# Last layer without its context rows, tokens kept on chip between two written-out layers, and modulation on four column tiles

## The chip, the cores and the metric

One Trainium2 chip, one core. The metric is the device time of one execution in microseconds (us); lower is better. In the traces PE is TensorE (matmuls; PEld its weight loads), DVE is VectorE, ACT is ScalarE, POOL is GpSimd and SP is SyncE, which here only issues DMAs.

## The reference

Two layers of a token mixer. 256 context tokens and 1024 latent tokens have 1024 channels each. A layer computes, with everything in float32:

```
for l in range(2):
    sh, sc, gt = split(silu(c) @ w_mod[l] + b_mod[l])          # latents; context tokens use silu(c_ctx)
    h = rmsnorm(x, norm_g[l]) * (1 + sc) + sh                  # ctx likewise
    p = h @ w_in[l]                                            # columns are split among the four head groups
    y = concat(diff_attention, mlstm, gla, window_gqa)         # each reads context and latents
    y = y * silu(p[gate columns])
    x = x + gt * (y @ w_out[l])
    if l == 0: ctx = ctx + gt_c * (yc @ w_out[l])              # only the first layer
return x
```

In the last layer the context tokens are keys, values and recurrent state for the latents. Their own mixed rows, gates and output are not used after it.

## The kernel before

Tokens come in NT = 10 tiles of 128: two of context (NC = 2), eight of latents. `hT` [128, 8, 1280] holds the modulated input by channel, `yT` of the same size the mixed output. Weights come as 18 slabs a layer through `ring`, two buffers of up to 2 MB (`load_slabs`, L158): SP loads slab i once slab i-2 has been used, which is counted in `slab_used`.

`layer_program` (L98) runs `setup`, and then a hardware loop over two layers. Each stage is a block of five programs, one for each engine, synchronized by semaphores, and a barrier of all engines that clears them ends it. The stages of a layer, in this order:

- `setup` (L175, once): loads the constants and c, copies the 5.24 MB of tokens from the input to the buffers `ctx_now` and `out` in DRAM, waits for all four transfers, and only then forms silu(c).
- `stage_modulation` (L204): SP loads the parameters `par` (1.18 MB), slabs 0 and 1, ten token tiles of 0.5 MB into `yT`, then slabs 2 to 7. PE multiplies each of slabs 0 to 5 (512 columns) by silu(c), 2 columns wide, in 8 float32 matmuls, which are 16 instructions (L241); ACT keeps each result (L262). Meanwhile ACT squares and sums the token tiles (L267), and ACT and DVE scale them (L277, L295). At the end PE turns the 2-row result into columns (L248), DVE adds the gate's bias (L300), PE spreads the gate rows over 128 partitions (L254), and ACT keeps them (L283).
- `stage_norm` (L314): PE transposes the scaled tokens (L346), ACT and DVE write `hT` with scale and shift.
- `stage_mlstm` and `stage_gla`, each closed by `turn_out` (L879), which normalizes the heads' rows and transposes them into `yT`, ten tiles.
- `stage_diff_attention` (L1565): projections, and for each of two pairs of heads `attend_pair` (L1583): 20 units (tile, head). Each unit has two score maps; DVE takes the maximum (L1719), ACT the exponential (L1690). A context tile has 256 keys, a latent tile 1280. Then `turn_out`.
- `stage_window_attention` (L1774): projections and 20 units (tile, group) of 256 to 640 keys (L1924 is the maximum).
- `stage_gates` (L1959): 5 groups of 256 gate columns, 8 steps (128 input channels) each. A step splits `hT` and the weights into high and low float32r parts (ACT L2023; DVE L353, L354, L2056) for PE, which does three matmuls (L2001 to L2003) for each of 2 column blocks by token blocks of 512, 512 and 256. A group has NA = 6 sums in a ring of 8 banks of PSUM: the first step of a group waits until sum n-8 has been read (`made`). ACT takes the sigmoid, DVE multiplies (L2040), POOL multiplies into `yT` (L2068).
- `stage_output` (L2074): 4 groups (column half, token half) of NA = 5 tiles, 8 steps each with 15 matmuls of 512 columns (L2120 to L2122). DVE multiplies the sum by the gate row (L2139), POOL adds it to the residual (L2164), ACT issues the store (L2170). The residual tiles come from DRAM through NB = 4 buffers: the load of tile i waits for the store of tile i-4 (L2106). 20 tiles of 256 KB.

All of this runs over all ten tiles in both layers.

## Time and profile before

| | us |
|---|---|
| median of 2 runs (2875.21 to 2882.43) | 2878.82 |
| the profiled execution, its device time | 2880.83 |
| the profiled execution, span from first to last instruction | 2878.9 |
| PE busy | 2266.4 (79%) |
| DVE busy | 1941.6 (67%) |
| ACT busy | 1203.8 (42%) |
| POOL busy | 426.7 (15%) |
| mean granted clock of TensorE, share of 2.4 GHz | 0.885 |

The device time is the metric; the profiled execution is one more run, 0.07% above the median, and its device time lies 1.9 us above its span. Busy shares are averages over stages that have different limits, so they say little of any one of them. The two layers run the same instructions: the first begins its modulation at 26.26 us and the second at 1452.71 us.

### The profile page before, as it was taken

What the parts mean: (1) busy time and instruction counts of PE and PEld (TensorE: products, weight loads), DVE (VectorE), ACT (ScalarE), POOL (GpSimd) and SP (SyncE); (2) the same over time, 40 slices, a digit from 0 to 9 for tenths busy, and PEclk for the clock granted to TensorE, in tenths of its full rate; (3) what the DMA queues carried; (4) which work ended last, traced back from release to release, by engine and by line L of the source; (5) the groups of instructions that cost most, each with busy time, mean ns of one, the idle gap of its engine ahead of it and who ended that gap; (6) DMA issues with size and microseconds to landing.
All of it is one profiled execution on the core that took longest, in us unless ns stands there. A gap on an engine that the chain in (4) does not pass through costs nothing. (4 is left out here: it accounts for less than half of the span.)

```text
span 2878.9 us, 39611 instructions
## 1 busy us (share of the span) xinstructions
PE 2266.4 (79%) x15156; PEld 1862.1 (65%) x15156; DVE 1941.6 (67%) x3585; ACT 1203.8 (42%) x2248; POOL 426.7 (15%) x422
## 2 busy tenths in 40 slices
PE   4877796786879758898958776977868787488988
PEld 0666685666768636777817666866657686377777
DVE  0476666778979467676715766677889686676766
ACT  2434343333757426442224433433437474364421
POOL 0001303322000030022200012042220000201212
PEclk9988897898989769999989888978989798699999
DMA  8200010000000100001271000100000001000022
GB/s 337 89 15 17 1 59 1 2 0 1 1 1 1 44 30 1 30 30 55 99 287 63 0 18 16 45 1 2 1 1 1 1 1 44 30 1 30 30 79 97
DMA packets 21041, 112.51 MB, mean 39 GB/s; under 512 B 2464, under 2 KB 2464, under 8 KB 15776
## 3 DMA queue, kind: packets, MB, share of 16 engines
q1 hardware_dynamic: 15088, 99.42, 9.2%
q10 hardware_dynamic: 5760, 10.49, 1.0%
q8 instruction: 124, 2.03, 0.3%
q14 instruction: 69, 0.57, 0.1%
HBM read 99.42 MB, written 15.73 MB: 40 GB/s over the span
## 5 line engine op out<-in xcount | busy, mean ns | idle before, releaser
L1719 DVE TENSOR_REDUCE a_st<-ps 128x1 f32<-128x1280 f32 (+1 forms) x160 | 203.5, 1274 | 24.0 <-PE ps L1631 23.1
L1690 ACT ACTIVATE ring<-ps,a_st 128x1280 f32<-128x1280 f32 (+1 forms) x160 | 184.7, 1155 | 76.9 <-DVE a_st L1719 76.3
L2001 PE MATMUL ps<-g_x_hi,g_w_hi 128*128 128x512 f32 (+1 forms) x480 | 175.8, 366 | 29.9 <-DVE g_gate L2040 15.4
L2002 PE MATMUL ps<-g_x_lo,g_w_hi 128*128 128x512 f32 (+1 forms) x480 | 174.8, 364 | 0.0
L2003 PE MATMUL ps<-g_x_hi,g_w_lo 128*128 128x512 f32 (+1 forms) x480 | 172.9, 360 | 0.0
L426 PE MATMUL ps<-a_proj_wh,a_proj_xh 128*128 128x512 f32 (+1 forms) x320 | 118.2, 369 | 65.7 <-DVE a_proj_xl L407 65.7
L2023 ACT ACTIVATE g_x_hi<-hT 128x1280 fp32r<-128x1280 f32 x80 | 101.4, 1272 | 146.3 <-PE ps L2003 139.8
L1631 PE MATMUL ps<-a_k,a_q 128*128 128x512 f32 (+1 forms) x416 | 131.0, 420 | 25.0 <-ACT ring L1690 20.4
L241 PE MATMUL ps<-ring,csil 128*2 128x512 f32 x192 | 92.1, 636 | 73.4 <-DMA ring<-in_w 72.5
L2056 DVE TENSOR_TENSOR g_x_lo<-hT,g_x_hi 128x1280 fp32r<-128x1280 f32 x80 | 119.1, 1489 | 29.4 <-ACT g_x_hi L2023 29.4
L2120 PE MATMUL ps<-o_w_hi,o_y_hi 128*128 128x512 f32 x320 | 125.9, 393 | 16.4 <-ACT o_y_hi L2176 16.4
L1646 PE MATMUL ps<-cst,ring 128*128 128x128 f32 x672 | 109.8, 295 | 29.4 <-ACT a_aT L1699 16.2
L2068 POOL TENSOR_TENSOR yT<-yT,g_gate 128x512 f32<-128x512 f32 (+1 forms) x60 | 66.1, 1124 | 449.5 <-DVE g_gate L2038 262.0
L2122 PE MATMUL ps<-o_w_hi,o_y_lo 128*128 128x512 f32 x320 | 125.5, 392 | 0.0
L2121 PE MATMUL ps<-o_w_lo,o_y_hi 128*128 128x512 f32 x320 | 125.5, 392 | 0.0
L2001 PEld LDWEIGHTS ps<-g_x_hi,g_w_hi 128*128 128x128 f32 x480 | 93.2, 194 | 49.3 <-DVE g_gate L2040 17.9
L390 ACT ACTIVATE b_proj_xh<-hT 128x640 fp32r<-128x640 f32 (+1 forms) x64 | 63.8, 1003 | 140.9 <-PE ps L426 138.5
L426 PEld LDWEIGHTS ps<-a_proj_wh,a_proj_xh 128*128 128x128 f32 x320 | 67.5, 211 | 78.7 <-issue 55.4
L2176 ACT ACTIVATE o_y_hi<-yT 128x640 fp32r<-128x640 f32 x64 | 47.0, 740 | 166.5 <-PE ps L2122 159.1
L426 PE MATMUL ps<-a_proj_wl,a_proj_xh 128*128 128x512 f32 (+1 forms) x320 | 115.2, 360 | 0.0
L426 PE MATMUL ps<-a_proj_wh,a_proj_xl 128*128 128x512 f32 (+1 forms) x320 | 114.7, 358 | 0.0
L1646 PEld LDWEIGHTS ps<-cst,ring 128*128 128x128 f32 x672 | 81.7, 151 | 49.2 <-ACT a_aT L1699 24.0
(358 smaller groups left out, 6533.4 us busy)
## 6 DMA issues: line engine op xcount, KB each, us to landing
ring<-in_w SPq DMA_DIRECT2D x26, 2048.0 KB, 7.6
yT<-latents SPq DMA_DIRECT2D x16, 512.0 KB, 18.6
o_res<-latents SPq DMA_DIRECT2D x32, 256.0 KB, 2.8
latents<-o_res ACTq DMA_DIRECT2D x32, 256.0 KB, 2.4
ring<-in_w SPq DMA_DIRECT2D x6, 1024.0 KB, 4.8
cst<-in_cst SPq DMA_DIRECT2D x1, 2752.0 KB, 8.9
ring<-in_w SPq DMA_DIRECT2D x2, 1312.0 KB, 5.5
par<-in_par SPq DMA_DIRECT2D x2, 1180.0 KB, 5.5
```

Of the source, the lines that this page charges most:

```text
L426: last = pe.matmul(out, left, right, start=k == 0 and j == 0, stop=k == KT - 1 and j == 2)
L1631: last = pe.matmul(ps[:, 3 * c + b, 0:w], q4[:, 2 * h + c, t * P:(t + 1) * P], k4[:, 2 * h + c, k0:k0 + w], start=True, stop=True)
L1646: last = pe.transpose(ps[:, 6 + n % 2, (k - a) * P:(k - a + 1) * P], p(u, 0, T)[:, k * P:(k + 1) * P], C(env, "ident"))
L1690: act.activation(p(u, c, n), ps[:, 3 * c:3 * c + 3, :].rearrange("p b n -> p (b n)")[:, 0:n], ACT.Exp, bias=st[:, 0:1], accum_out=st[:, 1: ...
L1719: dve.tensor_reduce(stat[:, u % SLOTS, c, 0:1], ps[:, 3 * c:3 * c + 3, :].rearrange("p b n -> p (b n)")[:, 0:n], AX.X, ALU.max, negate=Tru ...
L2001: pe.matmul(out, w_hi[:, at, cols], x_hi[:, at, toks], start=k == 0, stop=False)
L2002: pe.matmul(out, w_hi[:, at, cols], x_lo[:, at, toks], start=False, stop=False)
L2003: last = pe.matmul(out, w_lo[:, at, cols], x_hi[:, at, toks], start=False, stop=k == KT - 1)
L2056: dve.tensor_tensor(x_lo[:, at, :], hT[:, k, :], x_hi[:, at, :].bitcast(F32), ALU.subtract).then_inc(split_lo.sem, 1)
L2120: pe.matmul(ps[:, n % 8, :], y_hi[:, at, toks], w_hi[:, at, :], start=k == 0, stop=False)
L2121: pe.matmul(ps[:, n % 8, :], y_hi[:, at, toks], w_lo[:, at, :], start=False, stop=False)
L2122: last = pe.matmul(ps[:, n % 8, :], y_lo[:, at, toks], w_hi[:, at, :], start=False, stop=k == KT - 1)
```

## The change

1. The two layers are written out instead of looped over, and every address is a constant. Stage tensors and semaphores get the layer in their names.
2. In the last layer only the eight latent tiles are kept (`kept_tiles`): in `turn_out` (three times), the units of both attentions, the gates (1024 of 1280 token columns) and the output (8 of 10 tiles). The projections and the scans still run over all ten.
3. `setup` only loads c. The copy of the tokens in DRAM is gone. The first layer reads its tokens from the input, in modulation and again as residual. Order of SP's DMAs: slabs 0 and 1, ten token tiles, `par`, the constants, then slabs 2 to 7.
4. The output stage loads all its residual tiles at once into `hT` (by rows), each with a semaphore of its own, and POOL adds in place. They stay there, so the next layer's modulation reads them without a load; its scaled copy goes to `yT`.
5. In the first layer's output stage SP then loads the next `par`, slab 0 when the splits of the first column half are done, and slab 1 when those of the second are done.
6. Modulation: the eight matmuls of a slab are spread over four column tiles of the PE, k and k+4 sharing one. DVE clears two banks first; ACT keeps all 128 partitions. The turn becomes 16 float32 matmuls that also add the four partial rows (`pair_sum`), it waits for all six slabs, and the gate rows follow at once; their bias is added by DVE as it takes them from PSUM.
7. A second barrier at the end of each layer clears the slab semaphores.

```diff
-        with nc.Fori(0, DEPTH) as layer:
-            env["layer"] = layer
+        for layer in range(DEPTH):
+            env["layer"], env["last"] = layer, layer == DEPTH - 1
...
-                    first = loaded[0].sem.num if stage is stage_output else first_free
-                    nc.all_engine_barrier(sems_to_clear=range(first, first_free + len(stage_sems)))
+                    nc.all_engine_barrier(sems_to_clear=range(first_free, first_free + len(stage_sems)))
+                    if stage is stage_output:
+                        nc.all_engine_barrier(sems_to_clear=range(loaded[0].sem.num, slab_used.sem.num + 1))
...
+def kept_tiles(env):
+    return range(NC if env["last"] else 0, NT)
+def residual_rows(env, t, cols):
+    dram = env["dram"]
+    if env["layer"] == 0:
+        return dram["tok"][t * P:(t + 1) * P, cols]
+    return new_rows(env, t, cols)
...  setup
-            sp.dma_start(env["cst"][:, :], dram["cst"][:, :]).then_inc(const_loaded.sem, 16)
-            sp.dma_start(craw[:, :, :], dram["c"].rearrange("p (k c) -> p k c", k=KT)).then_inc(const_loaded.sem, 16)
-            sp.dma_start(dram["ctx_now"][:, :], dram["tok"][0:CTX, :]).then_inc(const_loaded.sem, 16)
-            sp.dma_start(dram["out"][:, :], dram["tok"][CTX:T, :]).then_inc(const_loaded.sem, 16)
-            sp.wait_ge(const_loaded.sem, 64)
+            sp.dma_start(craw[:, :, :], dram["c"].rearrange("p (k c) -> p k c", k=KT)).then_inc(c_loaded.sem, 16)
+            sp.wait_ge(c_loaded.sem, 16)
...  stage_modulation
+            if first:
+                load_slabs(sp, env, 0, 2)
+                for t in range(NT):
+                    sp.dma_start(x[:, t, :], env["dram"]["tok"][t * P:(t + 1) * P, :]).then_inc(x_loaded[t].sem, 16)
+                sp.dma_start(env["par"][:, :], env["dram"]["par"][0:P, :]).then_inc(par_loaded.sem, 16)
+                sp.dma_start(env["cst"][:, :], env["dram"]["cst"][:, :]).then_inc(env["const_loaded"].sem, 16)
             load_slabs(sp, env, 2, 8)
...
+            pe.wait_ge(cleared.sem, 2)
             for s in range(6):
-                pe.wait_ge(env["loaded"][s].sem, 16)
+                wait_slab(pe, s)
                 if s >= 2:
                     pe.wait_ge(ev.sem, s - 1)
                 for k in range(KT):
-                    last = pe.matmul(ps[0:2, s % 2, :], env["csil"][:, k, :], slab(env, s)[:, k, :],
-                                     start=k == 0, stop=k == KT - 1)
+                    c = k % 4
+                    last = pe.matmul(ps[32 * c:32 * c + 2, s % 2, :], env["csil"][:, k, :], slab(env, s)[:, k, :],
+                                     start=k < 4, stop=k >= 4, tile_position=(0, 32 * c), skip_group_check=True)
...
-            pe.wait_ge(ev.sem, 4)
+            pe.wait_ge(ev.sem, 6)
+            pe.wait_ge(env["const_loaded"].sem, 16)
             for i in range(2 * KT):
-                last = pe.transpose(ps[:, 2, 2 * i:2 * i + 2], rows[:, i * P:(i + 1) * P], C(env, "ident")[0:2, 0:2])
+                last = pe.matmul(ps[:, 2, 2 * i:2 * i + 2], rows[:, i * P:(i + 1) * P], C(env, "pair_sum"), start=True, stop=True)
...  stage_gates
-    NA = GROUP // P * len(BLOCKS)
+    blocks = [(CTX, 512), (CTX + 512, 512)] if env["last"] else BLOCKS
+    T0 = blocks[0][0]
+    NA = GROUP // P * len(blocks)
...
-                act.activation(x_hi[:, i % BUFS, :], hT[:, k, :], ACT.Copy).then_inc(split_hi.sem, 1)
+                act.activation(x_hi[:, i % BUFS, T0:], hT[:, k, T0:], ACT.Copy).then_inc(split_hi.sem, 1)
...  stage_output
-    NA = NT // 2
+    first = kept_tiles(env)[0]
+    NA = (NT - first) // 2
...
             for i, (n, t) in enumerate(jobs):
-                if i >= NB:
-                    sp.wait_ge(x_out[i % NB].sem, 16 * (i // NB))
-                sp.dma_start(res[:, i % NB, :], rows(n, t)).then_inc(x_in[i % NB].sem, 16)
+                sp.dma_start(xs[:, t, cols(n)], residual_rows(env, t, cols(n))).then_inc(x_in[i].sem, 16)
+            if not env["last"]:
+                nxt = slice((env["layer"] + 1) * P, (env["layer"] + 2) * P)
+                sp.dma_start(env["par"][:, :], dram["par"][nxt, :]).then_inc(ahead[0].sem, 16)
+                for i in range(2):
+                    sp.wait_ge(weights.sem, 2 * (i + 1) * KT)
+                    sp.dma_start(env["ring"][:, i, 0:KT * SLAB_W[i]], dram["w"][nxt, SLAB_AT[i]:SLAB_AT[i + 1]])\
+                      .then_inc(ahead[1 + i].sem, 16)
...  turn_out, attend_pair, stage_window_attention (one line of each)
-            for t in range(NT):
+            for i, t in enumerate(tiles):
-    units = [(t, h) for t in range(NT) for h in range(2)]
+    units = [(t, h) for t in kept_tiles(env) for h in range(2)]
-        pairs = [(t, g) for t in range(NT) for g in range(2)]
+        pairs = [(t, g) for t in kept_tiles(env) for g in range(2)]
```

## Rows read from the trace of the kernel before

**Rows 1.** SP's part of the timeline, start of each layer's modulation (start us, us, engine, line).

```profile
26.26 0.35 SPq L224 DMA_DIRECT2D par<-in_par  x1
...
1452.71 0.35 SPq L224 DMA_DIRECT2D par<-in_par  x1
```

**Rows 2.** Timeline of the setup and of layer 1's modulation end.

```profile
25.05 0.22 ACT L194 ACTIVATE csig<-craw 128x16 f32<-128x16 f32 x1 [23.02 <-DMA latents<-in_tok]
...
89.38 0.59 ACT L262 ACTIVATE mod_row<-ps 2x512 f32<-2x512 f32 x1 [6.75 <-PE ps L241]
...
99.00 10.80 PE L346 MATMUL ps<-cst,yT 128*128 128x128 f32 x80 [1.64 <-PEq L138]
```

**Rows 3.** Timeline of layer 2's modulation, 1440 to 1530 us.

```profile
1465.05 8.57 PE L241 MATMUL ps<-ring,csil 128*2 128x512 f32 x16 [22.41 <-DMA ring<-in_w]
...
1511.85 7.03 PE L241 MATMUL ps<-ring,csil 128*2 128x512 f32 x16 [0.31 <-DMA ring<-in_w]
...
1520.90 5.36 PE L254 MATMUL ps<-mod_row,cst 2*128 2x512 f32 x8 [0.76 <-DVE mod_row L300]
...
1527.90 2.37 PE L346 MATMUL ps<-cst,yT 128*128 128x128 f32 x10 [1.63 <-PEq L138]
```

**Rows 4.** Busy time by stretch, layer 2's modulation (stretch, length, engines, PE clock, DMA share, GB/s).

```profile
1474.00:1487.60 13.60, 6.79 (x16) 1.19 (x14) 0.17 (x1) 11.21 (x22) 0.00 (x0) 0.91 1.03 423
```

**Rows 5.** DMA issues of the page: size, median us from issue to landing.

```profile
ring<-in_w SPq DMA_DIRECT2D x26, 2048.0 KB, 7.6
```

**Rows 6.** Timeline: matmuls on two column tiles; weight loads before 64-column matmuls.

```profile
2589.95 1.09 PE L1874 MATMUL ps<-d_aT,d_v 128*64 128x128 f32 x16 [0.48 <-DVE yT L1944]
...
2365.63 2.31 PEld L1661 LDWEIGHTS ps<-yT,ring 128*128 128x128 f32 x20 [0.30 <-ACT a_aT L1699]
```

**Rows 7.** Timeline of differential attention: first maximum, first of a latent unit.

```profile
2149.79 0.76 DVE L1719 TENSOR_REDUCE a_st<-ps 128x1 f32<-128x256 f32 x2
...
2157.41 1.49 DVE L1719 TENSOR_REDUCE a_st<-ps 128x1 f32<-128x1280 f32 x1 [0.82 <-PE ps L1631]
```

**Rows 8.** Timeline of window attention: first maximum, first of a latent unit.

```profile
2499.66 0.42 DVE L1924 TENSOR_REDUCE d_st<-ps 128x1 f32<-128x256 f32 x1 [1.61 <-PE ps L1843]
...
2512.55 0.69 DVE L1924 TENSOR_REDUCE d_st<-ps 128x1 f32<-128x512 f32 x1 [0.39 <-PE ps L1848]
```

**Rows 9.** Timeline of the third turn_out: evictions of ten tiles.

```profile
2389.99 5.27 ACT L934 ACTIVATE yT<-ps,par 128x128 f32<-128x128 f32 x20 [1.24 <-PE ps L918]
```

**Rows 10.** Timeline of the last gates stage, and the start of the output stage.

```profile
2592.44 3.59 ACT L2023 ACTIVATE g_x_hi<-hT 128x1280 fp32r<-128x1280 f32 x3 [3.26 <-PEq L138]
...
2651.94 1.27 ACT L2023 ACTIVATE g_x_hi<-hT 128x1280 fp32r<-128x1280 f32 x1 [2.21 <-PE ps L2003]
...
2655.42 1.27 ACT L2023 ACTIVATE g_x_hi<-hT 128x1280 fp32r<-128x1280 f32 x1 [2.21 <-PE ps L2003]
...
2750.55 0.28 PE L2003 MATMUL ps<-g_x_hi,g_w_lo 128*128 128x256 f32 x1
...
2756.97 1.99 ACT L2176 ACTIVATE o_y_hi<-yT 128x640 fp32r<-128x640 f32 x3 [3.70 <-PEq L138]
```

**Rows 11.** Waits, 2592 to 2757 us: who waited for whom, total us, times, longest.

```profile
PE ps L2001 <- DVE g_gate L2040: 7.7, 3, 2.6
...
PE ps L2001 <- DVE g_gate L2038: 2.9, 2, 1.9
```

**Rows 12.** Costliest groups of the page: DVE's largest operation in the gates.

```profile
L2056 DVE TENSOR_TENSOR g_x_lo<-hT,g_x_hi 128x1280 fp32r<-128x1280 f32 x80 | 119.1, 1489 | 29.4 <-ACT g_x_hi L2023 29.4
```

**Rows 13.** Timeline of the last output stage's start and end.

```profile
2759.03 0.77 PE L2120 MATMUL ps<-o_w_hi,o_y_hi 128*128 128x512 f32 x1 [8.20 <-ACT o_y_hi L2176]
...
2869.02 0.39 PE L2122 MATMUL ps<-o_w_hi,o_y_lo 128*128 128x512 f32 x1
...
2874.24 1.26 POOL L2164 TENSOR_TENSOR o_res<-o_res,o_prod 128x512 f32<-128x512 f32 x1 [1.77 <-DMA o_res<-latents]
```

**Rows 14.** DMA queues of the page: instruction fetch (packets, MB, share).

```profile
q8 instruction: 124, 2.03, 0.3%
```

269 lines of the change are left out of this document (138 added, 131 removed).

## The prediction

> **What bounds the kernel now.** I read the timeline of SP first, because it cuts the run into two layers: modulation begins at 26.26 and again at 1452.71 us [rows 1]. The first layer takes 1426.5 us, and the second, up to the span's end at 2878.9, 1426.2: the same program twice, so a part that leaves one layer is priced from either. The chain of waits only covers the last output stage, so each changed stage is read by itself.
>
> *Setup.* ACT makes silu(c) at 25.05, released by the copy of the latents in DRAM [rows 2]: 25 us in which no engine computes. *Modulation.* PE's first matmul waits until 1465.05 for slab 0, 12.3 us after the stage's start. Then each slab takes 7.03 us of back-to-back matmuls with 0.31 us idle for the next load [rows 3]. PE and the two-slab ring are level, while a stretch where the queues are full moves 423 GB/s [rows 4]: a 2.10 MB slab needs 5.0 us of that, and the issue-to-landing time of 7.6 us [rows 5] leaves 2.6 us of fixed latency. *Gates and output.* In the gates a step comes every 3.48 us and ACT waits for PE each time [rows 10]; PE itself waits 10.6 us in all for DVE to free a bank [rows 11]. In the output stage 480 matmuls fill 2759.03 to 2869.4 without a gap, 3.41 us a step of 15 [rows 13]. Both are bound by PE, so fewer columns shorten them.
>
> **The change part by part.** The sum is made against the profiled execution's 2880.8 us (2.0 above the median).
>
> *Modulation's pace, p us of PE a slab.* The trace shows column tiles on two tiles only: 16 instructions of 128 columns take 1.09 us with the last one's own length in it, about 0.055 us apart [rows 6], while L241 needs 0.44 us for 512 columns on one, or 0.11 for 128 [rows 3]. Two tiles double the pace. Four would give 1.8 us a slab if all overlap, 3.5 if only two at a time do, and twice either at the low clock. The slab matmuls that followed an idle stretch took 8.57 us instead of 7.03, the first ones at half the pace [rows 3]. I take 3.5, with 1.8 and 6.9 as ends.
>
> *Layer 2's modulation.* No token loads, and slabs 0 and 1 are there: slab 1 is issued when DVE has split the last weights, three steps or 10 us before the output's PE end, and needs 7.6. From the start: 1.2 us for DVE's two clears (no row; two reads of 512 columns of PSUM are of that size; 0.3 to 1.2), slab 0 done at 4.7, slab 1 at 8.2. Slab 2 is issued at 4.7 and lands at 12.3, slab 3 5.0 later at 17.3. Slab 4 waits for slab 2's use at 15.8 and lands at 23.4; slab 5 lands at 28.4 and is used up at 31.9. Before, it was at 1518.9, or 66.2. That gives 34.3 us less (38.8 at p = 1.8, 22 at 6.9). ACT's ten squares and two copies, 11.2 us [rows 4], no longer begin behind slab 0's 21 us, and end near 16 us, ahead of slab 4; they hold nobody.
>
> *Layer 1.* c's load is 8 KB, so 2.6 us of latency after 0.8 of issue, and 1.2 us from silu(c) to the stage, as now (25.05 to 26.26): start at 4.6. Ahead of slab 2 lie 4.2 + 5.2 + 1.2 + 2.8 = 13.5 MB. The constants now count here instead of in setup. Slab 2 lands at 4.6 + 2.6 + 15.6 MB / 423 GB/s = 44.0, slab 3 at 49.0, slab 4 (issued at 47.5) at 55.1, slab 5 at 60.1, used up at 63.6. Before it was 89.3 [rows 2]: 25.7 less (28.5 and 17 at the ends of p).
>
> *End of modulation, both layers.* From the last slab to the norm's first transpose: 9.0 us in layer 2 (1518.9 to 1527.9 [rows 3]), 9.7 in layer 1 [rows 2]. The turn is now 32 instructions that each load 128x128 weights. Such loads come every 0.115 us at the full clock [rows 6], so 3.7 us, or 7.4 at half. The 8 gate instructions take 3.4 to 6.9 (5.36 in [rows 3]). With 0.7 for ACT's copy before, 0.7 for DVE's sum after and 1.2 of barrier that is 9.7 to 16.9. I take 13.3, since PE will have been idle half the time: 4.0 us dearer in each layer. PE's gate matmuls no longer wait for DVE's bias, which was 1 us of the old 9.
>
> *Transition.* All residual tiles are there early, so POOL's last add no longer waits 1.77 us for a load, which itself waited for a store [rows 13]: 1.9 us less in layer 1. SP's 20 loads, `par` and slab 0 go past nobody: the output stage's only other DMAs are ACT's stores. The second barrier costs about the 1.3 us that one takes between stages. The loop's own end shows no gap of its own.
>
> *Gates, last layer.* A step has 12 matmuls of 512 instead of 7680 columns: 0.8 x 3.48 = 2.78 us, 27.8 us less in 40 steps. NA = 4 in 8 banks means that a group's first step waits for the group before the last, long read, so the 10.6 us of bank waits go. DVE's largest part shrinks from 1.49 to 1.19 us [rows 12] of a 2.78 us step. At the end four sums at POOL's pace instead of six save about 0.7. Together 39 us. Ends: 28 if the bank waits stay, 40.
>
> *Output, last layer.* 32 steps of 12 instead of 15 matmuls: 32 x 0.68 = 21.8. The end: 9.5 us from the last matmul (2869.4) to 2878.9. New: the first of four sums is ready 2.0 us before PE's end, 0.7 for DVE, four adds of 1.26 [rows 13], and 3.4 us of store as now: 7.1. With 0.2 of smaller splits 24.4 us.
>
> *Attention, last layer.* Four units fall away at the front of each loop. Differential: 2157.41 - 2149.79 = 7.6 [rows 7], less 0.9 for the longer first scores, 6.7, twice: 13.4. Window: 12.9 - 0.9 = 12.0 [rows 8]. *turn_out*, three times: 4 of 20 evictions are 1.05 us [rows 9], and the squares ahead of them, by the same share, about as much again: 5.7 (3.2 to 6.3).
>
> *Sum.* 25.7 - 4.0 + 34.3 - 4.0 + 1.9 - 1.3 + 39 + 24.4 + 13.4 + 12.0 + 5.7 = 147.1. 2880.8 - 147.1 = **2734 us**, 5.1% faster. Some 94 us come from the dropped context rows and 53 from loads and modulation; the tiles alone would be worth little without the loads, since the ring's transfers would take PE's place at 5 us a slab.
>
> **The rivals.** *A: PE stays the bound of modulation.* With idle gaps between slabs PE may run at the low clock all through, and only two tiles may overlap: p = 6.9, so 12.3 us of layer 2's gain and 8.7 of layer 1's are lost, and the end takes 3.6 more in each: 2734 + 28 = 2762. For it: the clock was low in the first matmuls after the idle wait [rows 3]. Against: full clock for most of a stage with short gaps.
> The Trainium skill ("TensorE: Matmul & The Clock Gate", Part 1) says that the throttled state is the default and activity releases it; by that rule layer 2's modulation would be at 1.2 GHz for its whole length. The trace agrees for the stage's start and has no stage with half-idle PE for the rest.
> *B: the last layer's gates and output shrink less than their columns.* If DVE or ACT became the bound in the gates, or bank waits stayed, 11 to 28 us of the 39 would be missing: 2745 to 2762. Against: 1.19 of 2.78 us.
> *C: slower than before, by instruction fetch.* Twice the code, straight through. The fetch queue moves 124 packets [rows 14]. If each now stalled its engine by a landing of 2.6 us, that would be 322 us: 2734 + 322 = 3056. It decides against the change from 147 / 124 = 1.2 us a packet on. Against: a loop's first pass also runs code for the first time, and it took 1426.5 us where the second took 1426.2 [rows 1]; and 2.03 MB fetched is the code of both passes, not of one.
> The skill's page "Runtime: NRT & Kernel Launch", "Instruction fetch mechanics", has straight code prefetched and a far taken branch paying a fetch, so written-out layers would if anything save one such stall; no gap in this trace shows it.
> *D: the change does more.* p = 1.8, a full clock at the end of modulation and shorter attention fill: 2734 - 16 = 2718.
>
> **How the numbers follow.** Forecast as priced 0.62, A 0.16, B 0.10, D 0.10, C 0.01, anything else 0.01. The likeliest case lies within 2722 to 2748. The range takes in D and A: 2713 to 2765; C and a heavier mix of A and B are left out. No change from the median, within 2% (about what a measurement of this kernel can tell from none), begins at 2821 us, which only a sum below 60 us reaches, less than the dropped columns alone give: faster 0.97, same 0.02, slower 0.01.
>
> **What would show it.** Norm's first transpose at about 77 us (before 99.0) and, in layer 2, 45 us after its modulation's start (before 75.2). Slabs of modulation 5.0 us apart with PE waiting for DMA between them. The mixer stages of layer 1 unchanged. Gates 125 us in the last layer (before 164.5), steps of 2.78 us and no PE wait for L2040. Output 97.5 us (before 122). The first maximum of a latent unit follows the scores at once. Wrong would be: PE waits of another kind at the slabs, DVE late in the last gates, idle times named "issue" spread over layer 2.

## The result, and the profile after

The changed kernel took 2726.17 us (median of 2 runs, 2724.24 to 2728.10), the kernel before 2878.82: a ratio of 0.9468, 95% interval 0.9433 to 0.9503. The forecast was 2734 us. The profiled execution took 2724.24 us with a span of 2722.4, which is 156.5 us less than the span before; the prediction's sum was 147.1.

Cut at the first instruction of each stage that it priced, the two spans differ like this. Each length is the difference of two starts in the timelines.

```
stretch                                        before    after   measured  predicted
start to norm's first transpose, layer 1         99.0     78.5     -20.6     -21.7
from there to layer 2's modulation             1353.7   1349.5      -4.3      -0.6
layer 2's modulation, to the norm                75.2     45.7     -29.5     -30.3
from there to the last gates (norm, mixers)    1064.5   1024.4     -40.1     -31.1
last gates                                      164.5    125.1     -39.4     -39.0
last output stage                               121.9     99.3     -22.6     -24.4
sum                                                             -156.5    -147.1
```

**Start of layer 1.** The timeline of the start answers to [rows 2]. Its columns are as there.

```profile
2.38 0.22 ACT L216 ACTIVATE csig<-craw 128x16 f32<-128x16 f32 x1 [0.36 <-DMA craw<-in_c]
...
10.75 1.89 PE L270 MATMUL ps<-ring,csil 128*2 128x512 f32 x8 [10.75 <-DMA ring<-in_w]
...
42.67 3.59 PE L270 MATMUL ps<-ring,csil 128*2 128x512 f32 x16 [25.20 <-DMA ring<-in_w]
...
59.77 3.59 PE L270 MATMUL ps<-ring,csil 128*2 128x512 f32 x16 [3.08 <-DMA ring<-in_w]
64.08 6.99 PE L278 MATMUL ps<-cst,mod_row 128*128 128x2 f32 x32 [0.72 <-ACT mod_row L290]
70.92 5.73 PE L283 MATMUL ps<-mod_row,cst 128*128 128x512 f32 x8
78.45 1.72 PE L376 MATMUL ps<-cst,yT 128*128 128x128 f32 x12 [1.79 <-PEq L142]
```

The activation of silu(c) comes at 2.38 instead of 25.05 us. Slab 2 was forecast at 44.0 and is there at 42.67; slab 5 was to be used up at 63.6 and is at 59.77 + 3.59 = 63.4. PE now waits for a DMA ahead of each of these slabs. From slab 5's end to the norm 13.3 us were forecast; it is 78.45 - 63.36 = 15.1, with the 32 turning instructions at 6.99 us, near the prediction's price at half clock (7.4).

**Layer 2's modulation.** PE's timeline answers to [rows 3].

```profile
1428.98 3.59 PE L270 MATMUL ps<-ring,csil 128*2 128x512 f32 x16 [9.09 <-DVE ps L314]
1432.75 2.28 PE L270 MATMUL ps<-ring,csil 128*2 128x512 f32 x16 [0.18 <-PE ps L270]
1440.11 3.36 PE L270 MATMUL ps<-ring,csil 128*2 128x512 f32 x16 [5.08 <-DMA ring<-in_w]
1444.98 1.90 PE L270 MATMUL ps<-ring,csil 128*2 128x512 f32 x16 [1.51 <-DMA ring<-in_w]
1452.00 3.59 PE L270 MATMUL ps<-ring,csil 128*2 128x512 f32 x16 [5.12 <-DMA ring<-in_w]
1456.88 3.59 PE L270 MATMUL ps<-ring,csil 128*2 128x512 f32 x16 [1.29 <-DMA ring<-in_w]
1461.19 4.18 PE L278 MATMUL ps<-cst,mod_row 128*128 128x2 f32 x32 [0.72 <-ACT mod_row L290]
1465.23 6.60 PE L283 MATMUL ps<-mod_row,cst 128*128 128x512 f32 x8
1473.63 9.37 PE L376 MATMUL ps<-cst,yT 128*128 128x128 f32 x80 [1.79 <-PEq L142]
```

The stage starts at 1427.90 with DVE's first clear. Counted from there slabs 2 to 5 are there at 12.2, 17.1, 24.1 and 29.0 us (forecast 12.3, 17.3, 23.4, 28.4), and slab 5 is used up at 32.6 (31.9). Slab 4 comes 7 us after slab 3, not 5, because the two-slab ring lets SP issue it only when slab 2 is used. A slab takes one of two times, 3.59 or 1.90 us, or something between: the same 16 instructions at the low or the full level of PE's clock, 1.2 or 2.4 GHz. The gate rows answer to the 5.36 us of [rows 3] with 6.60.

**Gates and output of the last layer.** Busy time by stretch, with PE's clock, DMA share and GB/s last; then the waits of the gates; then the end of PE and POOL; then the page's row of fetched instructions.

```profile
2498.00:2624.00 126.00, 112.67 (x480) 91.29 (x480) 100.74 (x142) 54.57 (x63) 26.00 (x20) 0.96 0.13 51
2624.00:2722.40 98.40, 89.54 (x384) 72.79 (x384) 70.31 (x111) 19.14 (x31) 21.09 (x16) 0.97 0.24 86
...
PE ps L2033 <- DVE g_x_lo L2088: 8.6, 5, 3.9
...
2713.99 4.96 POOL L2205 TENSOR_TENSOR hT<-hT,o_prod 128x512 f32<-128x512 f32 x4 [13.95 <-DVE o_prod L2180]
...
2714.83 0.39 PE L2163 MATMUL ps<-o_w_hi,o_y_lo 128*128 128x512 f32 x1
...
q8 instruction: 119, 1.95, 0.3%
```

The bank waits of [rows 11] are gone. But PE waits 8.6 us for DVE's split tokens, of which 3.9 are the start of the stage (4.3 before): so in four other places PE waits 4.7 us that it did not wait before. The tail from PE's end to the span's end is 2722.4 - 2715.2 = 7.2 us (forecast 7.1, before 9.5). 119 packets of instructions were fetched, against 124 in [rows 14], though the second layer now has code of its own.

### The profile page after: what moved, and what is told of

It reads as the page before. It is cut to its first block and busy times, and to the rows that moved or that the text cites. A ratio compares the mean times of both kernels' runs of the same rounds, so it can differ in the third digit from the quotient of the medians.

```text
span 2722.4 us, 38298 instructions
## 1 busy us (share of the span) xinstructions
PE 2132.7 (78%) x14712; PEld 1782.9 (65%) x14712; DVE 1898.9 (70%) x3481; ACT 1160.6 (43%) x2144; POOL 413.2 (15%) x408
## 5 line engine op out<-in xcount | busy, mean ns | idle before, releaser
L2033 PE MATMUL ps<-g_x_hi,g_w_hi 128*128 128x512 f32 (+1 forms) x400 | 151.5, 379 | 23.5 <-DVE g_x_lo L2088 12.9
L456 PE MATMUL ps<-a_proj_wh,a_proj_xh 128*128 128x512 f32 (+1 forms) x320 | 117.4, 367 | 63.6 <-DVE a_proj_xl L437 63.4
L2055 ACT ACTIVATE g_x_hi<-hT 128x1280 fp32r<-128x1280 f32 (+1 forms) x80 | 92.9, 1166 | 137.9 <-PE ps L2035 131.4
L2034 PE MATMUL ps<-g_x_lo,g_w_hi 128*128 128x512 f32 (+1 forms) x400 | 150.4, 376 | 0.0
L2035 PE MATMUL ps<-g_x_hi,g_w_lo 128*128 128x512 f32 (+1 forms) x400 | 149.9, 375 | 0.0
L2088 DVE TENSOR_TENSOR g_x_lo<-hT,g_x_hi 128x1280 fp32r<-128x1280 f32 (+1 forms) x80 | 108.4, 1355 | 20.7 <-ACT g_x_hi L2055 20.6
L2162 PE MATMUL ps<-o_w_lo,o_y_hi 128*128 128x512 f32 x288 | 113.8, 395 | 0.0
L2163 PE MATMUL ps<-o_w_hi,o_y_lo 128*128 128x512 f32 x288 | 113.6, 394 | 0.0
L456 PE MATMUL ps<-b_proj_xh,b_proj_wh 128*128 128x512 f32 (+1 forms) x192 | 78.2, 407 | 43.9 <-DVE b_proj_xl L437 39.7
L420 ACT ACTIVATE a_proj_xh<-hT 128x640 fp32r<-128x640 f32 x64 | 46.7, 741 | 150.8 <-PE ps L456 148.6
L1676 PEld LDWEIGHTS ps<-cst,ring 128*128 128x128 f32 x656 | 79.2, 150 | 47.6 <-ACT a_aT L1729 23.4
L2218 ACT ACTIVATE o_y_hi<-yT 128x640 fp32r<-128x640 f32 (+1 forms) x64 | 43.5, 686 | 154.0 <-PE ps L2163 145.7
## 6 DMA issues: line engine op xcount, KB each, us to landing
cst<-in_cst SPq DMA_DIRECT2D x1, 2753.0 KB, 22.4
```

What stands on the lines that cost most here:

```text
L420: act.activation(self.x_hi[:, i % self.BUFS, 0:m], self.env["hT"][:, k, t0:t0 + m], ACT.Copy).then_inc(self.hi.sem, 1)
L456: last = pe.matmul(out, left, right, start=k == 0 and j == 0, stop=k == KT - 1 and j == 2)
L1676: last = pe.transpose(ps[:, 6 + n % 2, (k - a) * P:(k - a + 1) * P], p(u, 0, T)[:, k * P:(k + 1) * P], C(env, "ident"))
L2033: pe.matmul(out, w_hi[:, at, cols], x_hi[:, at, toks], start=k == 0, stop=False)
L2034: pe.matmul(out, w_hi[:, at, cols], x_lo[:, at, toks], start=False, stop=False)
L2035: last = pe.matmul(out, w_lo[:, at, cols], x_hi[:, at, toks], start=False, stop=k == KT - 1)
```

## The experiments

All ratios are to the kernel before, timed on the same chip, with their 95% intervals. A difference of two medians below some 7 us says little: the changed kernel itself gave 2726.17 and, timed again, 2732.45, and it was not timed again on the chips of the later runs. So each edit is read in its own stage too. The stretch that I use most is the one from the end of DVE's last product in layer 1's output stage (1422.5 us in the changed kernel) to the first operation of layer 2's first mixer, which holds the second modulation and the norm. "The output stage's last product" below is that point. In the changed kernel it took 62.0 and 60.7 us, in four other kernels that leave it alone 60.5 to 64.1, and 95.6 before.

### The changed kernel again

> The changed kernel again, as the control that the three beside it are read against. My theory and every rival: 2726 us, as before, within 0.3%.

2732.45 us, ratio 0.948 (0.9448 to 0.9512), span 2729.2. Of the 6.8 us between this span and the first one, 5.0 lie between the start of the first mixer's row sums (239.4 against 239.5 us) and its norm (326.0 against 321.1 us) in layer 1, where the code is the same. PE was busy there for 77.8 instead of 71.2 us with the same 760 matmuls, and up to 321.1 us its granted clock was 0.89 instead of 0.96. So this difference is the clock's.

### All ten token tiles kept in the last layer

```diff
-        return range(NC if env["last"] else 0, NT)
+        return range(0, NT)
-    blocks = [(CTX, 512), (CTX + 512, 512)] if env["last"] else BLOCKS
+    blocks = BLOCKS
```

> The changed kernel with one part taken out: the last layer works on all ten token tiles to its end, as the kernel before did. The loads kept ahead, the tokens kept on chip and the column tiles stay. The steps of the prediction that came from dropping context rows (gates 39, output 24.4, diff attention 13.4, window attention 12.0, turning out 5.7: 94.5 us together) must come back: 2726 + 94 = 2820 us, last gates 164 us and output stage 122 us again. Rival, that writing the layers out is what made part of these stages shorter (no loop, other instruction fetch): less than 80 us comes back, and the gates stay under 155 us although they work on 1280 columns. Rival, that the stages after the gates were shorter for another reason, such as their own waits for loads: the output stage stays near 100 us.

2823.0 us, ratio 0.9788 (0.9755 to 0.9821): 90.6 us more than the changed kernel beside it, and 58.3 less than the kernel before. The prediction had divided its sum as 94 and 53. Busy time by stretch for the last gates and output, and the waits of these gates:

```profile
2538.20:2702.50 164.30, 144.66 (x720) 121.07 (x720) 111.26 (x150) 65.87 (x71) 33.02 (x30) 0.96 0.10 39
2702.50:2824.70 122.20, 111.90 (x480) 92.13 (x480) 80.00 (x116) 23.48 (x32) 26.29 (x20) 0.95 0.24 87
...
PE ps L2033 <- DVE g_gate L2072: 7.7, 3, 2.6
PE ps L2033 <- DVE g_gate L2070: 2.9, 2, 1.9
```

Both stages have the lengths of before (164.5 and 121.9) within 0.3 us, and the bank waits are the same to the tenth as in [rows 11]. Neither rival holds. The mixers of layer 2 (first operation of the first one to the start of the gates) take 1046.4 us here, 1013.5 in the changed kernel (1016.5 when it was run again) and 1051.6 before.

### Layers written out, nothing else

```diff
-        with nc.Fori(0, DEPTH) as layer:
+        for layer in range(DEPTH):
             env["layer"] = layer
```

> The kernel before with its layer loop written out and nothing else changed: every load, tile and wait as it was, the instructions of the second layer stand behind those of the first. My theory holds that a written-out layer costs nothing measurable, since the fetch of instructions runs beside the work: 2878.8 us within 3 us, perhaps 1 to 2 us less for the loop's own branch. Rival C of the prediction, with a price of 2.6 us for each additional instruction packet: several per cent slower, up to 3200 us. Rival, that the changed kernel gained by being written out (better fetch, no barrier at the loop's end): 2865 us or less.

2881.65 us, ratio 1.0001 (0.9985 to 1.0018). Within 5 us either way, writing the layers out is worth nothing and costs nothing. Rival C is dead, and so is the idea that the changed kernel gained by it. It fetched 122 packets of instructions (queue 8 of its page).

### The column tiles alone, in the kernel before

The gate rows' bias moves to DVE's copy out of PSUM too, as in the changed kernel.

```diff
-                    last = pe.matmul(ps[0:2, s % 2, :], env["csil"][:, k, :], slab(env, s)[:, k, :],
-                                     start=k == 0, stop=k == KT - 1)
+                    c = k % 4
+                    last = pe.matmul(ps[32 * c:32 * c + 2, s % 2, :], env["csil"][:, k, :], slab(env, s)[:, k, :],
+                                     start=k < 4, stop=k >= 4, tile_position=(0, 32 * c), skip_group_check=True)
...
+                dve.memset(ps[:, b, :], 0.0).then_inc(cleared.sem, 1)
...
-                last = pe.transpose(ps[:, 2, 2 * i:2 * i + 2], rows[:, i * P:(i + 1) * P], C(env, "ident")[0:2, 0:2])
+                last = pe.matmul(ps[:, 2, 2 * i:2 * i + 2], rows[:, i * P:(i + 1) * P], C(env, "pair_sum"), start=True, stop=True)
```

> The kernel before with the column tiles of the modulation and their turn alone: loop, setup, token loads and all ten tiles as they were. The prediction said that the tiles alone would be worth little, since the ring's transfers take PE's place at 5 us a slab: by its own terms (7.0 - 5.0) x 4 slabs less the dearer end of 4.0, so 4 us a layer and 2871 us. Its rival, now the likelier to me since taking the tiles away cost 21 us in the two layers (7.8 to the first mixer in layer 1, 13 in layer 2): slab 0's 8.6 us shrink as well and the second slab's use comes earlier, so that the ring turns sooner: 8 to 10 us a layer, 2858 to 2862 us. Rival, that PE at the low clock is as slow as before: within 3 us of before.

2863.92 us, ratio 0.9946 (0.9930 to 0.9963), so 16 us faster, less than the 2% that counts as faster but clear of its interval. PE's timeline of layer 2's modulation, slabs 0, 2 and 5, and then slab 2 in the kernel before:

```profile
1453.48 3.58 PE L244 MATMUL ps<-ring,csil 128*2 128x512 f32 x16 [22.18 <-DMA ring<-in_w]
...
1475.99 3.59 PE L244 MATMUL ps<-ring,csil 128*2 128x512 f32 x16 [15.79 <-DMA ring<-in_w]
...
1494.20 3.39 PE L244 MATMUL ps<-ring,csil 128*2 128x512 f32 x16 [3.19 <-DMA ring<-in_w]
...
1487.65 9.21 PE L241 MATMUL ps<-ring,csil 128*2 128x512 f32 x16 [6.86 <-DMA ring<-in_w]
```

From slab 0's first matmul to slab 5's end it is 1497.6 - 1453.5 = 44.1 us instead of 1518.9 - 1465.1 = 53.8 [rows 3]. All of that comes behind slab 2's landing, which is as late as before: 22.5 us after slab 0's first matmul, against 22.6. So my rival, that a shorter slab 0 turns the ring sooner, does not hold. Slabs 2 to 5 take 21.6 us instead of 31.2. The first mixer begins 5.3 us earlier in layer 1, and the stretch in layer 2 is 87.8 instead of 95.6. So 13 us show in the two stages, more than the 8 that the prediction's terms give.

### One column tile in the changed kernel

The first piece of the diff above, turned round; clears and turn stay as they are.

> The changed kernel with the modulation's matmuls on one column tile again, one chain of eight after the other, everything else as in it. The prediction gave a slab on four tiles p = 3.5 us of PE; in the trace after it took 3.3 to 3.6 at the low clock and 1.9 at the full one, against 6.9 before. By my theory PE becomes the bound of both modulations: in layer 1 slabs 2 to 5 then arrive at 5.0 us and are used at 6.9, so 6 x 6.9 = 41 us end to end instead of some 28 to 30, in layer 2 41 + start instead of 33.8: 2727 + 8 to 14 for each layer = 2743 to 2755 us. Rival, that the loads kept ahead did it all and the tiles are worth nothing: within 3 us of the changed kernel.

2743.46 us, ratio 0.9549 (0.9516 to 0.9582). PE's timeline of layer 2's modulation, then busy time by stretch in the middle of it:

```profile
1443.39 7.03 PE L269 MATMUL ps<-ring,csil 128*2 128x512 f32 x16
...
1481.44 3.73 PE L277 MATMUL ps<-cst,mod_row 128*128 128x2 f32 x32 [0.69 <-ACT mod_row L289]
...
1440.00:1460.00 20.00, 19.24 (x45) 3.56 (x44) 0.17 (x1) 13.74 (x26) 0.00 (x0) 1.00 0.60 224
```

The same stretch in the changed kernel:

```profile
1440.00:1460.00 20.00, 11.97 (x64) 1.56 (x64) 4.26 (x10) 13.96 (x20) 0.00 (x0) 0.68 0.89 353
```

PE is busy from slab to slab at full clock and the DMA engines idle 40% of the time; with four tiles it is the other way round. The first mixer begins 7.6 us later in layer 1 (97.0 against 89.4), and the stretch in layer 2 takes 74.8 us, 12.8 to 14.1 more: some 21 us, the middle of what was expected. The medians show 11 to 17. The rival that the loads did it all falls. Against 7.03, four tiles take 1.90 us at the same clock: 3.7 times the pace.

### No slabs loaded ahead

SP loads slabs 0 and 1 when layer 2's modulation begins.

```diff
-                for i in range(2):
-                    sp.wait_ge(weights.sem, 2 * (i + 1) * KT)
-                    sp.dma_start(env["ring"][:, i, 0:KT * SLAB_W[i]], dram["w"][nxt, SLAB_AT[i]:SLAB_AT[i + 1]])\
-                      .then_inc(ahead[1 + i].sem, 16)
```

> The changed kernel without the two slabs that the output stage of the first layer loads ahead: SP issues slabs 0 and 1 of the second layer when its modulation begins. By the prediction's sum the modulation is bound by the arrival of slabs at 5.0 us each after a latency of 7.6: with six to come instead of four, 2 x 5.0 = 10 us more and PE's work on the last one unchanged, so 2736 us, less what PE held ready. Rival, that PE is the bound there: 7.6 us, the latency of the first slab alone. Rival, that ACT's and DVE's work on the tokens (squares, root, scaling) is what ends last in the second layer: less than 3 us.

2733.5 us, ratio 0.951 (0.948 to 0.954), which alone decides nothing. The stretch took 67.0 us, 5.0 to 6.3 more than in the changed kernel: below the rival's 7.6 and half of my 10. PE's timeline:

```profile
1434.11 3.41 PE L270 MATMUL ps<-ring,csil 128*2 128x512 f32 x16 [15.63 <-DMA ring<-in_w]
...
1445.04 3.60 PE L270 MATMUL ps<-ring,csil 128*2 128x512 f32 x16 [4.23 <-DMA ring<-in_w]
```

Slab 2 is there 1445.04 - 1421.1 = 23.9 us after the output stage's last product, with slabs ahead 1440.11 - 1422.5 = 17.6. In both it is issued when slab 0 has been used and is there 7.4 to 7.5 us later. So having slabs 0 and 1 saves the wait for slab 0 alone, here 1434.11 - 1421.1 = 13.0 against 6.5 us. My expectation forgot the ring, which the prediction's sum had in it.

### Tokens loaded again in layer 2

ACT waits for each of them again before it squares it.

```diff
+            else:
+                for t in range(NT):
+                    sp.dma_start(x[:, t, :], new_rows(env, t, slice(0, D))).then_inc(x_loaded[t].sem, 16)
             load_slabs(sp, env, 2, 8)
```

> The changed kernel with the second layer's tokens loaded from memory again (ten loads of 512 KB) ahead of slab 2, as the kernel before did, though they are on chip. The prediction held that what counts is the queue of bytes ahead of the last slab: ten tiles of 0.5 MB are 5.2 MB at 423 GB/s = 12.4 us more before slab 5 is there: 2727 + 12 = 2739 us. Rival, that the slabs go by other engines than the tokens and these cost only their issue: 2 to 3 us. Rival, that the squares that wait for the tokens end last then and cost more than the slabs: 15 to 20 us.

2736.8 us, ratio 0.9523 (0.9496 to 0.955). The stretch took 71.0 us, 9.0 to 10.3 more. SP's queue (eight of the ten loads) and the slab behind it:

```profile
1421.44 4.82 SPq L259 DMA_DIRECT2D hT<-latents  x8
...
1441.56 3.60 PE L273 MATMUL ps<-ring,csil 128*2 128x512 f32 x16 [14.35 <-DMA ring<-in_w]
```

Slab 2 is 26.2 us behind the output stage instead of 17.6. The theory of bytes ahead of the last slab holds in kind. It is 2 to 3 us too dear. The trace suggests why: SP issues the first token load at 1420.58 us and slab 0 is used up at 1425.13, so 4.5 of the 12.4 us fill a time in which the queue would stand empty, and 7.9 are left where slab 2 is 8.6 later. No run separates this from other reasons.

### Setup as before, in the changed kernel

```diff
             sp.dma_start(craw[:, :, :], dram["c"].rearrange("p (k c) -> p k c", k=KT)).then_inc(c_loaded.sem, 16)
-            sp.wait_ge(c_loaded.sem, 16)
+            sp.dma_start(dram["ctx_now"][:, :], dram["tok"][0:CTX, :]).then_inc(c_loaded.sem, 16)
+            sp.dma_start(dram["out"][:, :], dram["tok"][CTX:T, :]).then_inc(c_loaded.sem, 16)
+            sp.wait_ge(c_loaded.sem, 48)
```

(and the constants loaded there instead of ahead of slab 2)

> The changed kernel with the setup of before: SP loads the constants and copies the tokens from one place in memory to another, and the setup ends only when these have landed; the modulation's loads start after it. Layer 1's norm started 20.6 us earlier after the change, of which its tiles and the order of loads are a part. In the trace of before the setup took until some 30 us, in that of after until some 3. By my theory the setup's waits are worth more than all else at the start: 15 to 27 us, 2742 to 2754 us. Rival, that the start is bound by something in common (the loads of the first slabs would be as late without it): less than 6 us.

2743.86 us, ratio 0.9543 (0.9518 to 0.9569), 11 to 18 us more. PE's timeline:

```profile
33.18 3.59 PE L273 MATMUL ps<-ring,csil 128*2 128x512 f32 x16 [33.18 <-DMA ring<-in_w]
...
74.55 1.90 PE L273 MATMUL ps<-ring,csil 128*2 128x512 f32 x16 [1.37 <-DMA ring<-in_w]
77.16 4.63 PE L281 MATMUL ps<-cst,mod_row 128*128 128x2 f32 x32 [0.72 <-ACT mod_row L293]
```

PE's first matmul comes 22.4 us later, but slab 5 is used up only 76.5 - 63.4 = 13.1 us later, since the 2.8 MB of constants no longer stand ahead of slab 2. Of those 22 us the changed kernel keeps 13, less than the 15 to 27 that I had expected; and the norm starts only 11.1 earlier, because its turn runs at the low clock (6.99 us) and this one does not (4.63).

### Six, then five banks in the last gates

```diff
+    NBK = 6 if env["last"] else 8
...
-                    if k == 0 and n >= 8:
-                        pe.wait_ge(made.sem, n - 7)
-                    out = ps[:, n % 8, 0:b[1]]
+                    if k == 0 and n >= NBK:
+                        pe.wait_ge(made.sem, n - NBK + 1)
+                    out = ps[:, n % NBK, 0:b[1]]
```

> The changed kernel, with the last layer's gates going round six banks instead of eight, so that the third and fourth sum of a group must wait until the first two sums of the group before have been made. The steps and their work stay as they are. The prediction took 10.6 us of the gates' 39.5 from the vanished waits for banks (its size from the four waits in the trace of before). By that theory the waits come back on PE at the four group starts at some 2 to 3 us each: 2726 + 8 to 11 = 2734 to 2737 us. Rival, that the fall of the gates is all due to narrower steps and that the waits for banks lay beside DVE's own work, which would be late by as much anyway: 2726 to 2728 us, since DVE would catch up within the group.

2726.23 us, ratio 0.9468 (0.9437 to 0.9498). Nothing came back. PE's waits in the gates are those of the changed kernel:

```profile
PE ps L2034 <- DVE g_x_lo L2089: 8.6, 5, 3.9
```

The edit did not restore what I meant to test. With six banks a group waits only for sums that DVE makes in step 1 of the same group, and PE needs the bank just after that. In the kernel before, the last of four waiting sums waited for one made in step 2. Five banks restore that:

```diff
-    NBK = 6 if env["last"] else 8
+    NBK = 5 if env["last"] else 8
```

> The changed kernel with the last layer's gates going round five banks. With six nothing came back: in its trace the two sums that a group's third and fourth wait for were made 0.3 us before PE needed them. With five the fourth sum of a group also waits for the third of the group before, which DVE makes in step 2, some 3.8 us after PE would want the bank; that is the dependence that the kernel before had. In the changed kernel PE stands still for 1.6 to 2.2 us at each of these four places in another way, for DVE's split tokens, which are late since DVE makes four sums in steps 1 and 2. By the prediction's theory, that the bank waits are a cost of their own, some 2.6 us come back at each: 2727 + 10.6 = 2737 us. By the theory that I hold since six banks, DVE catches up while PE waits for the bank, and only the difference of 3.8 and 1.6 to 2.2 us comes back: 6 to 9 us, 2733 to 2736 us, the gates 131 to 134 us instead of 125. Rival, that the whole wait is DVE's lateness under another name: within 2 us, gates 125 to 127.

2733.26 us, ratio 0.9492 (0.947 to 0.9514). The last gates took 138.5 us instead of 125.1. PE's waits, and busy time by stretch over the 40 steps:

```profile
PE ps L2034 <- DVE g_gate L2073: 8.8, 3, 3.0
...
PE ps L2034 <- DVE g_x_lo L2089: 3.9, 1, 3.9
PE ps L2034 <- DVE g_gate L2071: 3.1, 1, 3.1
...
2494.00:2619.00 125.00, 111.74 (x450) 90.04 (x451) 94.49 (x134) 50.03 (x56) 20.92 (x16) 0.92 0.09 34
```

The same over the 40 steps with six banks:

```profile
2497.90:2609.30 111.40, 105.55 (x450) 85.78 (x451) 95.28 (x133) 49.92 (x56) 21.05 (x16) 0.97 0.10 38
```

PE now waits 11.9 us for banks, and the four waits for DVE's split tokens (4.7 us) are gone, as the theory of "only the difference" has it: 7.2 us. But the stage grew by 13.4, more than either theory had. The other 6.2 us are the clock: for the same 450 matmuls PE was busy 111.7 instead of 105.6 us, at a granted clock of 0.92 instead of 0.97. After three of the four waits matmuls follow each other at lower pace for a few microseconds (0.63 us long instead of 0.39). So a wait that was put in front of PE cost nearly twice its own length in this trace. It does not always: in the kernel before, with waits of up to 2.6 us at the same four places, only the first was followed by a lower clock (0.80 from 2627.4 to 2635.4 us), and in the kernel with the tiles alone, with the same waits, two were, and its gates took 167.3 us instead of 164.5. The prediction's flat 10.6 us was nearer in size than my second theory, for a reason that neither had.

### The turn behind slab 3

```diff
                 pe.sem_inc(env["slab_used"].sem, 1)
-            pe.wait_ge(ev.sem, 6)
-            pe.wait_ge(env["const_loaded"].sem, 16)
-            for i in range(2 * KT):
+                if s == 3:
+                    pe.wait_ge(ev.sem, 4)
+                    pe.wait_ge(env["const_loaded"].sem, 16)
+                    for i in range(2 * KT):
...
+                if s >= 4:
+                    n = s - 4
+                    pe.wait_ge(ev.sem, s + 1)
```

> The changed kernel with the turn of the modulation's rows into columns right behind slab 3 (its rows are those of slabs 0 to 3), and each half of the gate rows right behind slab 4 and slab 5, so that PE does them while it waits 5 us for a slab. In the changed kernel these stand behind slab 5: 6.99 and 5.73 us in layer 1, 4.18 and 6.60 us in layer 2. By my theory the turn goes off the path, as does half of the gate rows: 6.99 + 2.9 + 4.2 + 3.3 = 17 us less, minus some 3 us for DVE's sums that now end last: 2727 - 14 = 2713 us, ratio to the kernel before 0.942. Rival, that they delay the slabs behind them, for the slab's matmuls stand in the same queue: at most 5 us of gain. Rival, that DVE's or ACT's token work ends last: 8 us of gain.

2707.06 us, ratio 0.9408 (0.9392 to 0.9424), span 2698.9. PE's timeline in layer 2:

```profile
1437.51 3.92 PE L279 MATMUL ps<-cst,mod_row 128*128 128x2 f32 x32 [0.72 <-ACT mod_row L294]
1441.36 3.35 PE L270 MATMUL ps<-ring,csil 128*2 128x512 f32 x16
...
1447.35 1.90 PE L270 MATMUL ps<-ring,csil 128*2 128x512 f32 x16
1449.96 1.98 PE L287 MATMUL ps<-mod_row,cst 128*128 128x512 f32 x4 [0.72 <-ACT mod_row L294]
1453.74 9.36 PE L380 MATMUL ps<-cst,yT 128*128 128x128 f32 x80 [1.79 <-PEq L142]
```

From slab 5's end to the norm it is 1453.74 - 1449.25 = 4.5 us instead of 13.2. Slab 5 is used up as early as before the edit (38.1 us after the output stage's last product against 38.0), but 3.4 us later in layer 1 (66.8 against 63.4), which is all that is left of the rival of delayed slabs. The stretch took 53.5 us, 7 to 8.5 less, and layer 1's first mixer begins at 82.2 instead of 89.4: 14 to 16 us in the two stages, where 14 were expected. The medians show 19 to 25, and the rest of that I can't place. With the clock high again behind slab 5, half of the gate rows takes 1.98 us instead of 3.3.

### Constants split, and the gates of layer 1 a step earlier

```diff
-                sp.dma_start(env["cst"][:, :], env["dram"]["cst"][:, :]).then_inc(env["const_loaded"].sem, 16)
-            load_slabs(sp, env, 2, 8)
+                a, b, end = CST["sel_mod"][0], CST["pair_sum"][1], env["dram"]["cst"].shape[1]
+                sp.dma_start(env["cst"][:, a:b], env["dram"]["cst"][:, a:b]).then_inc(env["const_loaded"].sem, 16)
+            load_slabs(sp, env, 2, 6)
+            if first:
+                for lo, hi in ((0, a), (b, end)):
+                    sp.dma_start(env["cst"][:, lo:hi], env["dram"]["cst"][:, lo:hi]).then_inc(rest_loaded.sem, 16)
+            load_slabs(sp, env, 6, 8)
...
-                if g >= 1 and k in (1, 2):
+                if g >= 1 and k in (E0, E0 + 1):
```

> The same with two more edits, each of which shows in a stage of its own. First, of the 2.8 MB of constants only the 258 columns that the modulation needs are loaded ahead of slab 2, the rest behind slab 5: 2.7 MB at 423 GB/s are 6.3 us that slabs 2 to 5 of layer 1 arrive earlier, so its norm starts 5 to 6 us earlier than in the kernel with the early turn. Second, in the first layer's gates (whose sums still take six of eight banks a group) ACT and DVE make the gates in steps 0 and 1 instead of 1 and 2, so that the fourth sum's bank is free a step sooner: of the 10.6 us of bank waits up to 8 go, 165 to 157 us. Rival for the second: ACT's and DVE's splits for step 1 then come late, and PE waits for them instead: within 2 us of 165, or above. Together 2713 - 5.5 - 8 = 2700 us, or 2708 if the rival for the gates holds.

2698.83 us, ratio 0.9379 (0.9361 to 0.9396): the fastest of all, 8 us below the kernel with the early turn. Slab 2 in layer 1, and PE's waits in layer 1's gates:

```profile
36.38 3.59 PE L277 MATMUL ps<-ring,csil 128*2 128x512 f32 x16 [17.34 <-DMA ring<-in_w]
...
PE ps L2045 <- DVE g_x_lo L2100: 9.1, 5, 4.3
PE ps L2045 <- DVE g_gate L2084: 3.6, 3, 1.2
PE ps L2045 <- DVE g_gate L2082: 1.4, 1, 1.4
```

Slab 2 is there 6.6 us earlier than the 42.98 us of the kernel with the early turn (6.3 expected), and the first mixer 8.0. In the gates the rival holds: bank waits fell from 10.6 to 5.0 us, waits for split tokens rose by 4.8, and the stage went from 164.6 to 163.0. For that case 2708 us had been expected; the first mixer, 8.0 us earlier where some 5.5 were expected, and the 1.6 us of the gates explain about half of the rest. The two ends of DVE's work trade against each other.

## Why the prediction held, and where it did not

**Dropped context rows (94 us).** Right in sum: keeping the rows gives 90.6 back. Gates 39 (39.4), output 24.4 (22.6), mixers 31.1 (32.9 between the kernel with all rows and the changed one, 29.9 when it was run again). The gates' 39 is right by luck, by two errors that cancel. The waits fell by 5.9 us and not by 10.6: the bank waits went, but 4.7 us of another wait came. DVE, whose "largest part shrinks from 1.49 to 1.19 us" in the prediction, also makes four sums in two of eight steps, and is then too late with its splits. I had priced DVE's largest operation and not all that it issues in those steps. In return PE's own time between its first and last matmul fell by 32.2 us (144.9 to 112.7) and not by 27.8. A step is 2.72 us, not 2.78 (ACT's conversions follow at 2551.37, 2554.09 and 2556.81 us), because the six dropped matmuls of 256 columns had cost 0.76 us, more than half of six full ones; that is 2.4 us in 40 steps. The low clock behind the first bank wait (0.80 over 8 us), which is gone too, is another 1.6.

**The other 9 us.** The stretch from layer 2's norm to its gates fell by 40.1 us where 31.1 were forecast. 2.1 of it are the norm, whose 80 transposes took PE 9.37 us instead of 11.42; the mixers fell by 38.1. Differential attention, from its first maximum to its last, gave 18.6 for 13.4. Of this surplus 3.4 us lie between its two pairs of heads, where the work did not change: from the first pair's last maximum to the second pair's first it took 43.9 us before and 40.5 after. Busy time by stretch: the kernel before in layer 2, the same in its layer 1, and the changed kernel in layer 2.

```profile
2234.67:2278.57 43.90, 32.55 (x192) 28.33 (x190) 23.81 (x49) 16.16 (x33) 6.56 (x10) 0.77 0.00 1
...
809.68:847.64 37.96, 26.89 (x192) 22.75 (x190) 23.81 (x49) 16.23 (x33) 6.57 (x10) 0.91 0.00 1
...
2162.22:2202.69 40.47, 29.39 (x194) 25.37 (x193) 23.91 (x49) 16.16 (x33) 6.58 (x10) 0.86 0.00 1
```

The other engines' busy times agree within 0.1 us, and PE's time goes with its granted clock, 0.77, 0.91 and 0.86. At a like clock (0.91 in layer 1 of the kernel before, 0.90 in layer 2 of the changed kernel run again) the whole attention took 208.1 and 194.5 us: 13.6 apart, so by these traces the forecast of 13.4 was right and the surplus is the clock's. Whether the dropped rows bring the higher clock is not shown. In layer 1, whose code is the same in all kernels, this stretch had 0.91 to 0.95 in five traces and 0.76 or 0.77 in nine; in layer 2 it had 0.73 to 0.77 in the four traces with all rows and 0.80 to 0.96 in the ten without. The rest is no effect of the change that I can show: the mixers of layer 1 took 1045 to 1059 us over the fourteen traces, and layer 2's with dropped rows 1010 to 1020.

**Modulation (60 us, less 8 for its end).** 52 were forecast and 50.1 measured. The times of landing were right within 1.5 us, and so the step "the ring's two slabs, 7.6 us from issue to landing, 5.0 a transfer" holds. The pace p = 3.5 us was right in number and wrong in reason. I had read it as two tiles overlapping at the full clock; in fact all four overlap (1.90 us) and the clock is mostly low (3.59). Both gave the same sum, which is luck, and the low clock came back in the end of layer 1's modulation (15.1 for 13.3 us). Rival A had the clock right and the overlap wrong. The Trainium skill ("TensorE: Matmul & The Clock Gate", Part 1) has the throttled state as the default, which activity releases. As the prediction read that rule, every slab would have taken 3.59 us. The trace shows a granted clock of 0.71 over layer 2's stage, with slabs 1 and 3 at or near full, so it agrees only in part.

**The tiles alone.** "Would be worth little" was too small by a third in the two stages: 13 us instead of some 8 (16 between the medians). What failed is the 2 us that the terms gave each of slabs 2 to 5. In layer 2 the slabs behind slab 2 came 4.9, 6.6 and 6.7 us apart and not 5.0, which by itself is worth less. But the prediction had read 7.03 us for every slab behind the first, where slab 2, which follows a wait of 6.86 us, took 9.21; and the last slab's own use fell from 7.03 to 3.39. Together that is 9.6 us and not 8. The norm behind them was 1.4 us shorter in layer 1 and 2 in layer 2, which I had not priced. Taken from the changed kernel the tiles are worth 21 us, most of it in layer 2 (12.8 to 14.1 against 7.8 alone). I take the reason to be that slabs 0 and 1 are on chip there and no tokens stand in the queue ahead of slab 2.

**Setup.** The constants had to be counted ahead of slab 2, and were: 13.1 of 22.4 us are kept.

**Transition and instruction fetch.** The second barrier was priced at 1.3 us. From the end of POOL's last add to SP's first load of layer 2 it is 3.87 us before, with a loop and one barrier, 3.18 written out with one barrier, and 3.55 and 3.53 with two (the kernels without slabs ahead and with tokens reloaded). By these single traces the second barrier costs 0.4 us and the loop's end, which the prediction took for nothing, 0.7. Rival C fell with the ratio of 1.0001: also by the Trainium skill ("Runtime: NRT & Kernel Launch", "Instruction fetch mechanics") straight code is prefetched, and the experiment agrees. That the loop's 0.7 us are the stall of a taken branch, which that page of the Trainium skill has too, no run shows.

**Rivals B and D.** B named bank waits or DVE as the bound of the gates; a part of it is true (4.7 us), too little to show in the sum. D forecast more than the priced sum, and more came, but not for its reasons: in layer 2 p = 1.8 was the pace in two slabs of six, and gained nothing there, since PE waits for the next load anyway; and the end of modulation stayed at the low clock in part.

## What to carry to other kernels

When a stage's time is the last load's landing, work of another engine that stands behind the last use (a turn, a spread of rows) is worth as much as the loads: look for what can be done with the first slabs' results in the gaps, and split a large load so that only the part the stage needs goes first. Price a freed wait with what the same helper is late with next: put all that it issues in those steps beside the time of the engine that bounds the stage. Read a surplus against the same code elsewhere in the trace before you give it a cause: here layer 1 showed that five microseconds of attention were the clock's. And test a wait by restoring the same dependence, not just a smaller buffer; with six banks instead of five I had tested nothing.

## What the runs showed of the hardware

- Four column tiles of fp32 matmuls with 2 columns of weights and 512 moving ones overlap almost wholly: 1.90 us for 16 instructions against 7.03 on one tile at the same full clock, and 3.59 at the low one.
- Work that is nearly four times faster left PE idle, and the clock was lower: 0.68 of full in the middle of layer 2's stage, where one tile held 1.00. The gain on paper was 7.03 to 1.90 us; six of the changed kernel's twelve slabs got 3.59, and in layer 1 the turn behind them took 6.99 us instead of 3.73.
- The state of the clock at one point made a difference of its own: with the same code ahead of it, layer 1's turn took 6.99 us in the changed kernel and 4.01 in the one with tokens reloaded, and the norm began at 78.45 and 73.62 us.
- The same 192 matmuls between the two pairs of differential attention came with a stretch of 37.4 us at a granted clock of 0.95 and of 45.0 at 0.73; 0.95 and 0.77 both occur in layer 1, where all kernels have the same code.
- A wait in front of a busy PE can cost more than itself: with five banks 11.9 us of bank waits in four places (in place of 4.7 us of shorter waits) came with 6.2 us more of low clock. At the same places in the kernel before, 10.6 us of waits came with some 1.6.
- Two layers of straight code (38298 instructions executed in the changed kernel) need no more fetched packets than the loop did: 119 to 122 against 124.
